# Operands placed by their byte address, and four stage borders rearranged, in a hybrid encoder layer

## The chip, the core and the metric

The kernel runs on one core of a Trainium2 chip. The metric is the device time of one execution, in microseconds. TensorE (PE in the profile) multiplies, VectorE (DVE), ScalarE (ACT) and GpSimd (POOL) work element by element, SyncE (SP) mostly issues DMAs. Every engine has its own instruction queue, and they meet through semaphores.

## What is computed

One layer of a bidirectional encoder on 1280 tokens of width 1024 (1024 sample tokens and 256 prompt tokens), all in float32. Cut to what matters here:

```python
h  = rmsnorm(x, norm_mix)
q, k, v, g, r_f, r_b, aq, ak, av, z_a, z_b = split(h @ w_in)
o_a = gated_linear_attention(q, k, v, g, log_sigmoid(r_f @ w_gk_f + b_gk_f), log_sigmoid(r_b @ w_gk_b + b_gk_b))
o_b = attention(rope(rmsnorm(aq)), rope(rmsnorm(ak)), av)
merged = sigmoid(z_a) * (o_a @ w_o_gla) + sigmoid(z_b) * (o_b @ w_o_att)
x  = x + merged @ w_out
ht = rmsnorm(x, norm_ffn)
gate, idx = top_k(softmax(ht @ w_router).T, 2 * T / 16)     # each of 16 experts picks its tokens
xe  = ht[idx]
ye  = (silu(xe @ w_e_gate) * (xe @ w_e_up)) @ w_e_down * gate
y   = x + scatter_add(idx, ye)
```

r_f and r_b, 16 columns each, are called codes in the kernel.

## The kernel before

The stages run one after another, each in a block of its own with a barrier of all engines at its end: `project` (h and h @ w_in, 0 to 534 us of the profiled span), `gla` (534 to 932, with the z columns of w_in multiplied in between), `mix` with the tag mg (o_a @ w_o_gla, to 1058), `attention` (to 1348), `mix` with the tag ma (to 1464), `finish_mixer` (fm, to 1620), `choose` (tk, the top-k lists, to 1656) and `experts` (ex, to 3135). Names in the profile carry the stage's tag, as pj_w_hi or ex_xS.

A product that has to be exact to float32 is made of three passes: each factor is split into a high part in a type that TensorE takes at full rate (F32R, 4 bytes per element) and a low part, the rest. ACT writes the high part (a copy), DVE the low part (a subtraction), and PE multiplies high by high, high by low and low by high (`three_passes`, L107 to L111, and `channel_tile`, L114 to L131). act_hl holds both parts of the activations of all 1280 tokens. In token tiles (in `project`, the z work and `experts`) 128 tokens are the stationary operand and up to 512 weight columns move past it; in channel tiles (`channel_tile`) 128 weight columns stand still and the tokens move in blocks of 512, 512 and 256 (TOK3).

Where a tensor lies in SBUF follows from the sizes of what was allocated ahead of it: `Phase.sb` (L59) and `program` (L2220 on) take the next free multiple of 32 bytes from the left, or from the right end for those with side="right". Each tensor has the same address in all 128 partitions.

What orders the work around the change:

- `project`: PE ends with the codes, three blocks of tokens, then one ACT copy takes all of them out of PSUM (L412). SP's queue stores every tile and at its end waits for the stores.
- `gla`: SP's queue starts with `gate_weights(0)`, four small DMAs (L1113, L1114), `load_z(0)`, `load_qk(0)` and `ph.start(sp)`, for which other engines wait.
- `mix` mg: rows of o_a^T come in one by one into four buffers (two of them loaded ahead, in `gla`), ACT writes the high part of row k (L901), DVE the low part (L971), and PE's tile 0 waits for each row's low part (`ready` in `channel_tile`). SP loads row k again into the buffer of row k - 4 when its low part is done.
- `choose`: DVE makes the lists (its last step is L1896, slots_i); the first gather of tokens is Pool's first work in the block of `experts` behind it (`gather`, L1989 and L1993).
- `experts`: per expert Pool gathers the next expert's tokens, waits for the sample result (dve_s) and the prompt result (dve_p), and adds both to the output with indirect DMAs (L2010), y for the sample tokens first, then y_q. Weights come in through 8 raw buffers on SP's queue; ACT and DVE split them for the sample tokens (L2024, L2069), while the prompt tokens are multiplied with the raw weights (L2167).

```python
                gate_weights(0)
                load_z(0)
                load_qk(0)
                ph.start(sp)
```

Of the kernel before, what the change touches and what calls it, by code (L numbers as in the profile page):

```python
# [7 lines left out]
ALU = mybir.AluOpType  # L8
# [8 lines left out]
P = 128  # L17
# [33 lines left out]

class Phase:

    def __init__(self, nc, ctx, tag):
# [58 lines left out]
def channel_tile(pe, banks, w, act, full, ready=None, by_columns=False):  # L114
# [8 lines left out]
    for k in range(KC):  # L123
        if ready is not None:
            pe.wait_ge(ready, CR + k + 1)
# [13 lines left out]
def project(nc, x, w_cols, norm_mix, qk_norms, cos, sin, cst, ident, ident_in, act_hl, proj_t, proj_c, codes, ss):  # L139
# [3 lines left out]
    with ExitStack() as ctx:  # L143
# [8 lines left out]
        whi, wlo = ph.sb("w_hi", [P, 2, KC, UW], F32R), ph.sb("w_lo", [P, 2, KC, UW], F32R)  # L152
        rraw = ph.sb("r_raw", [P, KC, RC])
        rhi, rlo = ph.sb("r_hi", [P, KC, RC], F32R), ph.sb("r_lo", [P, KC, RC], F32R)
# [25 lines left out]
        squares = ph.sb("squares", [P, D])[:]  # L180
# [13 lines left out]
        with nc.Block() as block:  # L194

            @block.sync
            def _(sp):
# [117 lines left out]
            def _(act):  # L315
                def square(n, s, i):
# [3 lines left out]
                    act.activation(squares, xt[:, s], ACT.Square, accum_out=ssq[:, s:s + 1]).then_inc(squared, 1)  # L320
# [90 lines left out]
                act.wait_ge(p_full, CR + tok_n + chan_n + 1)  # L411
                act.activation(codes[:], ps_c[0:RC, 0].rearrange("p c n -> p (c n)")[:, 0:T], ACT.Copy).then_inc(p_out, 1)  # L412
# [62 lines left out]
            def _(pe):  # L475
# [60 lines left out]
                mm.then_inc(p_full, 1)  # L536
# [4 lines left out]
def attention(nc, proj_t, inv, cst, kT, vv, queries, act_hl, w_next, w_unit, w_landed):  # L541

    with ExitStack() as ctx:
        ph = Phase(nc, ctx, "at")
        qT = ph.sb("qT", [P, 2, AH, P], F32R)
        pT = ph.sb("pT", [P, 2, 2, NTS, 2, P], F32R)
# [236 lines left out]
def mix(nc, tag, act_hl, w, w_unit, z_rows, out, add=None, o=None, stored=None, source=None, rows_in=None, before=None, keys=None, follow=None, prepare=None):  # L784

    with ExitStack() as ctx:
        ph = Phase(nc, ctx, tag)
        raw, *whl = ([first, ph.sb(n, [P, KC, P], d)[:]] for first, n, d in zip(w_unit, ("w_raw", "w_hi", "w_lo"), (F32, F32R, F32R)))
# [22 lines left out]
        block_gated, block_done = ph.done("block_gated", "block_done")  # L811
# [7 lines left out]
        with nc.Block() as block:  # L819
# [54 lines left out]
            def _(act):  # L874
# [48 lines left out]
            def _(dve):  # L923
# [44 lines left out]
                if source is not None:  # L968
                    for k in range(KC):
                        dve.wait_ge(rows_hi, CR + k + 1)  # L970
                        dve.tensor_tensor(act_hl[:, 1, k], rows[k % NR], act_hl[:, 0, k].bitcast(F32), ALU.subtract).then_inc(rows_lo, 1)  # L971
# [36 lines left out]
            def _(pe):  # L1008
                for t, s in tiles:
# [3 lines left out]
                                 lambda j, k, a, b: act_hl[:, j, k, a:b], full, rows_lo if source is not None and t == 0 else None, by_columns=t == NT8 - 1)  # L1013
# [12 lines left out]
def gla(nc, proj_t, proj_c, z_c, o_t, w_z, wg, bg, g_norm, masks, codes, cst, act_hl, zraw, zw, w_next, qk, rows_in):  # L1026

    with ExitStack() as ctx:
        ph = Phase(nc, ctx, "gl")  # L1030
        v, g = ph.sb("v", [P, NT, DV]), ph.sb("g", [P, NT, DV])
        wgate, bias = ph.sb("w_gate", [3 * RANK, 2, DK]), ph.sb("bias", [P, 2])
# [15 lines left out]
        oss, oroot, oinv = (ph.sb(n, [P, 2]) for n in ("oss", "oroot", "oinv"))  # L1048
# [10 lines left out]
        const_in, qk_in, g_in, w_in, z_in = (ph.landed(n) for n in ("const_in", "qk_in", "g_in", "w_in", "z_in"))  # L1059
# [47 lines left out]
        with nc.Block() as block:  # L1107

            @block.sync
            def _(sp):  # L1110
                def gate_weights(i):
                    for d in range(2):
                        sp.dma_start(wgate[2 * RANK * d:2 * RANK * d + RANK, d], wg[d][:, bass.ds(i * DK, DK)]).then_inc(w_in, 16)  # L1113
                        sp.dma_start(bias[:, d:d + 1], bg[d].rearrange("o (p u) -> (o p) u", u=1)[bass.ds(i * DK, DK)]).then_inc(w_in, 16)  # L1114

# [22 lines left out]
                def body(i, last):  # L1138
                    m = 1 + ZM * i
                    if not last:  # L1140
                        sp.wait_ge(ring_out, CR + RING0 + RING * i)
                        gate_weights(i + 1)
# [52 lines left out]
                gate_weights(0)  # L1195
# [421 lines left out]
def finish_mixer(nc, x, merged, raw, w_in, first_parts, first_tile, merged_stored, norm_ffn, w_router, cst, y, h2, affT, vals, lists, idx):  # L1617

    with ExitStack() as ctx:
# [3 lines left out]
        whl = [(first, ph.sb(n, [P, KC, D // 2], F32R)) for first, n in zip(first_parts, ("w_hi", "w_lo"))]  # L1623
# [212 lines left out]
def choose(nc, affT, cst, vals, lists, idx, slots_i, slots_g, slots_q, start_counts, start_weights, first_high):  # L1836
# [4 lines left out]
    with ExitStack() as ctx:  # L1841
# [10 lines left out]
        with nc.Block() as block:  # L1852
# [45 lines left out]

            @block.scalar
# [12 lines left out]
def experts(nc, affT, vals, lists, idx, h2, y, w_gate, w_up, w_down, slots_i, slots_g, slots_q, cst):  # L1912

    with ExitStack() as ctx:
# [7 lines left out]
        raw = ph.sb("w_raw", [P, NRAW, 2, HF])  # L1923
        whl = [ph.sb(n, [P, NHL, 2, HF], F32R) for n in ("w_hi", "w_lo")]
# [29 lines left out]
        choose(nc, affT, cst, vals, lists, idx, slots_i, slots_g, slots_q, ph.start, start_weights, first_high)  # L1954
# [8 lines left out]
        with nc.Block() as block:  # L1963
# [22 lines left out]
            def _(pool):  # L1986
                def gather(e):
                    for j in range(2):
                        pool.tensor_copy(rows_x[j][:], slots_i[j][:, bass.ds(e, 1)]).then_inc(row_x, 1)  # L1989
                    pool.wait_ge(row_x, CR + 2 * e + 2)  # L1990
                    ph.settle(pool)
                    for j in range(2):
                        pool.indirect_dma_start(xe[j][:], None, h2, bass.IndirectOffsetOnAxis(ap=rows_x[j][:, 0:1], axis=0)).then_inc(x_in[j], 16)  # L1993

# [337 lines left out]
```

## Time and profile before

| | us |
|---|---|
| median of 3 executions | 3151.28 |
| lowest, highest | 3151.15, 3152.47 |
| the profiled execution | 3151.37 |
| its span, first to last instruction | 3149.8 |
| PE busy in the span | 3021.8 (96%) |
| DVE, ACT, POOL busy | 1715.3, 1521.5, 560.9 |
| mean granted clock of TensorE | 0.981 of full speed |

The span is the profiled execution without what lies around it, 1.6 us. A busy engine is one that has an instruction in flight; for PE two matmuls overlap in the records, so that a matmul's own duration is longer than the distance between the starts of two of them, and a span that is 96% busy says nothing about how fast the matmuls follow each other.

### The profile page before, as it was taken

How to read it: one execution, taken by the hardware profiler on the slowest of the kernel's cores; microseconds unless marked ns; L12 is line 12 of the kernel's file. 1: busy time of each engine (PE TensorE's matmuls, PEld its weight loads, DVE VectorE, ACT ScalarE, POOL GpSimd, SP SyncE). 2: the span in 40 equal slices, each digit the busy share in tenths (PEclk: the TensorE clock that was granted, in tenths of full speed). 3: DMA queues.
4: the chain of work that ended last, by engine and by line, in shares of the span. 5: the costliest groups of instructions: out<-in, count | busy, mean ns of one | idle time of the engine just before them, and what ended most of it. 6: DMA issues, size and time to landing. Idle time of an engine off the chain costs nothing. (4 is left out here: it accounts for less than half of the span.)

```text
span 3149.8 us, 51649 instructions
## 1 busy us (share of the span) xinstructions
PE 3021.8 (96%) x19370; PEld 2391.6 (76%) x19370; DVE 1715.3 (54%) x1748; ACT 1521.5 (48%) x1659; POOL 560.9 (18%) x729
## 2 busy tenths in 40 slices
PE   8999999999989999999949999999999999999998
PEld 6888886777778799878837777777777777777776
DVE  4101000555443599924367676666667676666665
ACT  4211111455632366622435665655666665556554
POOL 0048883112220000011100111000111100111100
PEclk9999999999999999999969999999999999999999
DMA  5224323233335100063447887778888778888874
GB/s 184 105 99 143 121 90 103 96 111 115 95 111 195 55 20 20 7 227 135 160 163 260 296 285 273 276 284 293 293 296 293 270 274 299 284 289 291 293 273 146
DMA packets 196414, 600.32 MB, mean 191 GB/s; under 512 B 15392, under 2 KB 45744, under 8 KB 196336
## 3 DMA queue, kind: packets, MB, share of 16 engines
q1 hardware_dynamic: 166144, 508.03, 44.9%
q0 software_dynamic: 21328, 73.41, 7.8%
q10 hardware_dynamic: 8864, 17.83, 1.6%
q8 instruction: 50, 0.82, 0.1%
q14 instruction: 28, 0.23, 0.0%
HBM read 521.80 MB, written 77.33 MB: 190 GB/s over the span
## 5 line engine op out<-in xcount | busy, mean ns | idle before, releaser
L2069 DVE TENSOR_TENSOR ex_w_lo<-ex_w_raw,ex_w_hi 128x2048 fp32r<-128x2048 f32 x384 | 880.0, 2292 | 451.1 <-ACT ex_w_hi L2024 451.1
L2024 ACT ACTIVATE ex_w_hi<-ex_w_raw 128x2048 fp32r<-128x2048 f32 x381 | 729.9, 1916 | 469.6 <-PE ex_ps_s L2156 469.5
L2156 PE MATMUL ex_ps_s<-ex_w_hi,ex_xS 128*128 128x512 f32 x2048 | 578.5, 396 | 0.0
L2156 PEld LDWEIGHTS ex_ps_s<-ex_w_hi,ex_xS 128*128 128x128 f32 x2048 | 376.2, 188 | 99.1 <-issue 26.3
L2156 PE MATMUL ex_ps_s<-ex_w_lo,ex_xS 128*128 128x512 f32 x1024 | 316.7, 390 | 0.0
L2156 PE MATMUL ex_ps_s<-ex_w_hi,ex_hidS 128*128 128x512 f32 x1024 | 308.1, 403 | 0.0
L2010 POOL DMA_INDIRECT y<-ex_ye_s,ex_rows_y x16 | 43.7, 2729 | 1147.1 <-DVE ex_ye_s L2112 1147.1
L2167 PE MATMUL ex_ps_p<-ex_w_raw,ex_xP 128*32 128x256 f32 x4096 | 236.1, 383 | 0.0
L2156 PEld LDWEIGHTS ex_ps_s<-ex_w_lo,ex_xS 128*128 128x128 f32 x1024 | 192.4, 188 | 41.3
L109 PE MATMUL pj_ps_tok<-pj_w_hi,act_hl 128*128 128x512 f32 x560 | 219.9, 393 | 2.4 <-DVE act_hl L436 2.4
L111 PE MATMUL pj_ps_tok<-pj_w_hi,act_hl 128*128 128x512 f32 x560 | 218.9, 391 | 0.0
L110 PE MATMUL pj_ps_tok<-pj_w_lo,act_hl 128*128 128x512 f32 x560 | 218.9, 391 | 0.0
L2156 PEld LDWEIGHTS ex_ps_s<-ex_w_hi,ex_hidS 128*128 128x128 f32 x1024 | 183.0, 188 | 46.6 <-issue 13.2
L2167 PEld LDWEIGHTS ex_ps_p<-ex_w_raw,ex_xP 128*32 128x32 f32 x4096 | 127.2, 110 | 100.5 <-issue 24.3
L453 DVE TENSOR_TENSOR pj_w_lo<-pj_w_raw,pj_w_hi 128x4096 fp32r<-128x4096 f32 x7 | 32.9, 4697 | 300.4 <-ACT pj_w_hi L363 300.4
L368 ACT ACTIVATE pj_stage<-pj_ps_tok 128x512 f32<-128x512 f32 x70 | 41.9, 598 | 287.3 <-PE pj_ps_tok L111 287.3
L2156 PE MATMUL ex_ps_s<-ex_w_lo,ex_hidS 128*128 128x512 f32 x512 | 159.6, 393 | 0.0
L109 PE MATMUL gl_z_ps<-act_hl,z_w_hi 128*128 128x512 f32 (+1 forms) x384 | 152.0, 396 | 0.4 <-issue 0.4
L111 PE MATMUL gl_z_ps<-act_hl,z_w_lo 128*128 128x512 f32 (+1 forms) x384 | 138.2, 360 | 0.0
L110 PE MATMUL gl_z_ps<-act_hl,z_w_hi 128*128 128x512 f32 (+1 forms) x384 | 137.7, 358 | 0.0
L109 PEld LDWEIGHTS pj_ps_tok<-pj_w_hi,act_hl 128*128 128x128 f32 x560 | 105.7, 189 | 24.9 <-DVE act_hl L436 3.1
L111 PEld LDWEIGHTS pj_ps_tok<-pj_w_hi,act_hl 128*128 128x128 f32 x560 | 105.6, 189 | 22.0
(334 smaller groups left out, 5140.1 us busy)
## 6 DMA issues: line engine op xcount, KB each, us to landing
ex_w_raw<-w_e_gate SPq DMA_DIRECT2D x128, 1024.0 KB, 11.3
ex_w_raw<-w_e_up SPq DMA_DIRECT2D x128, 1024.0 KB, 11.7
ex_w_raw<-w_e_down SPq DMA_DIRECT2D x128, 1024.0 KB, 8.7
proj_t<-pj_stage SPq DMA_DIRECT2D x60, 256.0 KB, 2.1
pj_w_raw<-w_cols ACTq DMA_DIRECT2D x7, 2048.0 KB, 8.8
z_w_raw<-w_z SPq DMA_DIRECT2D x16, 512.0 KB, 4.0
gate_logits<-gl_z_stage SPq DMA_DIRECT2D x32, 256.0 KB, 2.1
pj_w_raw<-x SPq DMA_DIRECT2D x10, 512.0 KB, 3.7
```

Source lines behind the costliest of these rows:

```text
L109: pe.matmul(out, a[0], b[0], start=first, stop=False)
L110: pe.matmul(out, a[0], b[1], start=False, stop=False)
L111: return pe.matmul(out, a[1], b[0], start=False, stop=last)
L368: act.activation(stage[:, s, 0:width], src, ACT.Copy).then_inc(p_out, 1)
L453: dve.tensor_tensor(wlo[:, s], raw[:, s], whi[:, s].bitcast(F32), ALU.subtract).then_inc(w_lo, 1)
L2010: pool.indirect_dma_start(dst, bass.IndirectOffsetOnAxis(ap=rows_y[j][:, 0:1], axis=0), src[:], None, compute_op=ALU.add).then_inc(scatter ...
L2024: act.activation(whl[0][:, j % NHL], raw[:, j % NRAW], ACT.Copy).then_inc(w_hi, 1)
L2069: dve.tensor_tensor(whl[1][:, j % NHL], raw[:, j % NRAW], whl[0][:, j % NHL].bitcast(F32), ALU.subtract).then_inc(w_lo, 1)
L2156: mm = pe.matmul(ps_s[:, s, c:c + 512], x(part, k), whl[w][:, j % NHL, kk, c:c + 512], start=k == 0 and part + w == 0, stop=k == 2 * PU - ...
L2167: mm = pe.matmul(ps_p[CP * c:CP * c + CP, f % 2, 0:QW], x(k, c), raw[:, j % NRAW, k % 2, QW * c:QW * c + QW], start=k == 0, stop=k == 2 * ...
```

## The change

1. **Places.** `place` puts every tensor of at least 512 bytes per partition at a chosen offset within 128 bytes, with a gap tensor ahead of it where needed: activations at 0 (AT), weights and other partners of a product at 64 (AT_W; also kT and pT in `attention`). The right end is shifted so that the tensors there lie at 64. `gla`'s own tensors are packed as before (lines=False). To free space `project` loses its buffer squares (the Square writes into xn instead, behind one more wait) and `gla` merges three small tensors.
2. **Codes by blocks.** PE reports each of the three code blocks, and ACT copies each by itself.
3. **First gate weights.** The four DMAs of `gate_weights(0)` go into `project`'s SP queue, behind its last store and ahead of its last waits.
4. **Row 0 by blocks.** In mg ACT and DVE split row 0 in three column blocks, and PE takes row 0 block by block, all three passes of a block together.
5. **First gather.** It goes into a Pool block of `choose`, behind a wait for the last list.
6. **Scatter.** The prompt's scatter goes first as soon as dve_p is there, then the sample's on dve_s.

The core of the diff:

```diff
@@ placement
+BYTES = {F32: 4, F32R: 4, U32: 4, BF16: 2, U8: 1}
+LINE, AT, AT_W = 128, 0, 64
+
+def place(nc, ctx, name, shape, dt=F32, at=AT):
+    size = math.prod(shape[1:]) * BYTES[dt]
+    if size >= 512 and at is not None:
+        gap = (at - (nc.sbuf_base + 31) // 32 * 32) % LINE
+        if gap:
+            ctx.enter_context(nc.sbuf_tensor(f"gap_{name}", [P, gap // 4], F32))
+    return ctx.enter_context(nc.sbuf_tensor(name, shape, dt))
+
 class Phase:
-    def sb(self, name, shape, dt=F32):
-        return self.ctx.enter_context(self.nc.sbuf_tensor(f"{self.tag}_{name}", shape, dt))
+    def sb(self, name, shape, dt=F32, at=AT):
+        return place(self.nc, self.ctx, f"{self.tag}_{name}", shape, dt, at if self.lines else None)
@@ project
-        whi, wlo = ph.sb("w_hi", [P, 2, KC, UW], F32R), ph.sb("w_lo", [P, 2, KC, UW], F32R)
+        whi, wlo = ph.sb("w_hi", [P, 2, KC, UW], F32R, AT_W), ph.sb("w_lo", [P, 2, KC, UW], F32R, AT_W)
...
+                first_gates(sp, 0)
                 for s in range(2):
                     sp.wait_ge(stored[s], ST + 16 * (tok_n + chan_n) // 2)
...
+                    act.wait_ge(turned, CR + n - 1)
-                    act.activation(squares, xt[:, s], ACT.Square, accum_out=ssq[:, s:s + 1]).then_inc(squared, 1)
+                    act.activation(xn[:, s], xt[:, s], ACT.Square, accum_out=ssq[:, s:s + 1]).then_inc(squared, 1)
...
-                act.wait_ge(p_full, CR + tok_n + chan_n + 1)
-                act.activation(codes[:], ps_c[0:RC, 0].rearrange("p c n -> p (c n)")[:, 0:T], ACT.Copy).then_inc(p_out, 1)
+                for c, (a, b) in enumerate(TOK3):
+                    act.wait_ge(p_full, CR + tok_n + chan_n + c + 1)
+                    act.activation(codes[:, a:b], ps_c[0:RC, 0, c, 0:b - a], ACT.Copy).then_inc(p_out, 1)
...
-                mm.then_inc(p_full, 1)
+                    mm.then_inc(p_full, 1)
@@ channel_tile, mix
+        if ready is not None and k == 0:
+            for c, (a, b) in enumerate(TOK3):
+                pe.wait_ge(ready[0] if b < T else ready[1], CR + c + 1 if b < T else CR + 1)
+                three_passes(pe, banks[:, c, 0:b - a], (w(0, k), w(1, k)), (act(0, k, a, b), act(1, k, a, b)), True, False)
+            continue
...
-                        act.activation(act_hl[:, 0, k], rows[k % NR], ACT.Copy).then_inc(rows_hi, 1)
+                        for c, (a, b) in enumerate(TOK3 if k == 0 else [(0, T)]):
+                            act.activation(act_hl[:, 0, k, a:b], rows[k % NR][:, a:b], ACT.Copy).then_inc(rows_hi if b == T else row0_hi, 1)
...
+                        for c, (a, b) in enumerate(TOK3 if k == 0 else [(0, T)]):
+                            dve.wait_ge(rows_hi if b == T else row0_hi, CR + k + 1 if b == T else CR + c + 1)
+                            dve.tensor_tensor(act_hl[:, 1, k, a:b], rows[k % NR][:, a:b], act_hl[:, 0, k, a:b].bitcast(F32),
+                                              ALU.subtract).then_inc(rows_lo if b == T else row0_lo, 1)
@@ gla
-        ph = Phase(nc, ctx, "gl")
+        ph = Phase(nc, ctx, "gl", lines=False)
...
-                gate_weights(0)
                 load_z(0)
                 load_qk(0)
                 ph.start(sp)
@@ choose, experts
+            @block.gpsimd
+            def _(pool):
+                pool.wait_ge(out, CR + 10)
+                first_gather(pool, 0)
...
-        raw = ph.sb("w_raw", [P, NRAW, 2, HF])
-        whl = [ph.sb(n, [P, NHL, 2, HF], F32R) for n in ("w_hi", "w_lo")]
+        raw = ph.sb("w_raw", [P, NRAW, 2, HF], F32, AT_W)
+        whl = [ph.sb(n, [P, NHL, 2, HF], F32R, AT_W) for n in ("w_hi", "w_lo")]
...
-                    pool.wait_ge(dve_s, CR + 3 * e + 3)
-                    pool.wait_ge(dve_p, CR + 3 * e + 3)
-                    ph.settle(pool)
-                    for j, (dst, src) in enumerate(((y, yS), (y_q, yP))):
+                    for j, dst, src, ready in ((1, y_q, yP, dve_p), (0, y, yS, dve_s)):
+                        ph.settle(pool)
+                        pool.wait_ge(ready, CR + 3 * e + 3)
+                        ph.settle(pool)
                         pool.indirect_dma_start(dst, bass.IndirectOffsetOnAxis(ap=rows_y[j][:, 0:1], axis=0), src[:], None,
                                                 compute_op=ALU.add).then_inc(scattered[j], 16)
...
-                gather(0)
                 experts_of(pool, body)
@@ program
+        gap = (nc.sbuf_top - AT_W) % LINE
+        if gap:
+            ctx.enter_context(nc.sbuf_tensor("gap_right", [P, gap // 4], F32, side="right"))
...
-            act_hl = mixer.enter_context(nc.sbuf_tensor("act_hl", [P, 2, KC, T], F32R))
             ss = mixer.enter_context(nc.sbuf_tensor("head_squares", [P, NT, HEADS], F32))
+            act_hl = place(nc, mixer, "act_hl", [P, 2, KC, T], F32R)
...
-                kT = kvs.enter_context(nc.sbuf_tensor("kT", [P, 2, KVH, T], F32R))
-                vv = kvs.enter_context(nc.sbuf_tensor("vv", [P, 2, NT, KVH * HD], F32R))
+                kT = place(nc, kvs, "kT", [P, 2, KVH, T], F32R, AT_W)
+                vv = place(nc, kvs, "vv", [P, 2, NT, KVH * HD], F32R)
```

In the same way AT_W is given to pj_r_hi and r_lo, at_pT, the `mix` weights, fm's w_hi and w_lo; the other tensors named in `program` (codes, w_gate, gate_bias, head_inverses, q_rows, affT, aff, lists, idx) go through `place` with AT.

## Rows read from the trace of the kernel before

**Rows 1.** Stages: stretch us, busy us of PE PEld DVE ACT POOL, PEclk, DMA share, GB/s.

```profile
549.00:932.00 383.00, 362.29 (x1844) 295.39 (x1843) 196.51 (x357) 205.10 (x351) 74.67 (x84) 0.99 0.31 101
932.00:952.00 20.00, 13.53 (x54) 10.90 (x54) 9.65 (x7) 8.79 (x7) 2.15 (x4) 0.74 0.85 325
1058.00:1348.00 290.00, 271.14 (x1874) 243.48 (x1872) 256.85 (x462) 186.92 (x382) 22.26 (x18) 0.98 0.07 21
1656.00:3135.00 1479.00, 1479.00 (x11314) 1098.30 (x11312) 1019.09 (x622) 880.06 (x603) 149.18 (x154) 1.00 0.79 280
```

**Rows 2.** Timeline of PE: start us, duration us, line, operands; token part of project.

```profile
200.33 0.39 PE L109 MATMUL pj_ps_tok<-pj_w_hi,act_hl 128*128 128x512 f32 x1
...
205.77 0.39 PE L109 MATMUL pj_ps_tok<-pj_w_hi,act_hl 128*128 128x512 f32 x1
```

**Rows 3.** Chain that ended last, the 20 longest pieces: start us, length us, what.

```profile
1661.71 11.10 PE ex_ps_s L2156 x48
```

**Rows 4.** Groups by form in experts: busy us, mean ns of one, idle before.

```profile
L2156 PE MATMUL ex_ps_s<-ex_w_hi,ex_xS 128*128 128x512 f32 x2048 | 578.5, 396 | 0.0
L2156 PE MATMUL ex_ps_s<-ex_w_lo,ex_xS 128*128 128x512 f32 x1024 | 316.7, 390 | 0.0
L2156 PE MATMUL ex_ps_s<-ex_w_hi,ex_hidS 128*128 128x512 f32 x1024 | 308.1, 403 | 0.0
...
L2156 PE MATMUL ex_ps_s<-ex_w_lo,ex_hidS 128*128 128x512 f32 x512 | 159.6, 393 | 0.0
```

**Rows 5.** Timeline of PE, last tile of the first mix.

```profile
1043.98 0.39 PE L109 MATMUL mg_ps<-act_hl,mg_w_hi 128*128 128x512 f32 x1
...
1046.78 0.40 PE L109 MATMUL mg_ps<-act_hl,mg_w_hi 128*128 128x512 f32 x1
```

**Rows 6.** Timeline of PE, last tile of the second mix.

```profile
1449.38 0.40 PE L110 MATMUL ma_ps<-act_hl,ma_w_hi 128*128 128x512 f32 x1
...
1451.48 0.39 PE L110 MATMUL ma_ps<-act_hl,ma_w_hi 128*128 128x512 f32 x1
```

**Rows 7.** Timeline of PE, scores in attention.

```profile
1199.89 0.39 PE L109 MATMUL at_ps_scores<-kT,at_qT 128*128 128x512 f32 x1
...
1201.06 0.40 PE L111 MATMUL at_ps_scores<-kT,at_qT 128*128 128x512 f32 x1
```

**Rows 8.** Groups by form, token part of project (one of three passes).

```profile
L109 PE MATMUL pj_ps_tok<-pj_w_hi,act_hl 128*128 128x512 f32 x560 | 219.9, 393 | 2.4 <-DVE act_hl L436 2.4
```

**Rows 9.** Timeline of all engines, project to gla; idle time before and its releaser in brackets.

```profile
533.73 1.23 ACT L412 ACTIVATE codes<-pj_ps_chan 48x1280 f32<-48x1280 f32 x1 [10.92 <-PE pj_ps_chan L111]
535.84 0.37 SPq L1113 DMA_DIRECT2D gl_w_gate<-w_gk_f  x1
...
537.65 0.43 SPq L1125 DMA_DIRECT2D z_w_raw<-w_z  x1
...
539.47 1.19 PE L1499 MATMUL gl_ring<-codes,gl_w_gate 16*128 16x512 f32 x1 [5.78 <-SPq L84]
```

**Rows 10.** Timeline of all engines, tile 0 of the first mix.

```profile
952.76 1.43 PE L128 MATMUL mg_ps<-act_hl,z_w_hi 128*128 128x512 f32 x6 [1.43 <-DVE act_hl L971]
953.01 1.27 ACT L901 ACTIVATE act_hl<-mg_row 128x1280 fp32r<-128x1280 f32 x1 [1.83 <-DMA mg_row<-gla_out]
```

**Rows 11.** Timeline of all engines, choose to experts.

```profile
1646.02 0.17 DVE L1896 TENSOR_TENSOR slots_i<-tk_diff,tk_b 128x16 uint32<-128x16 f32 x1
1647.11 0.29 POOL L1989 COPY ex_rows_x<-slots_i 128x1 uint32<-128x1 uint32 x2 [67.57 <-POOLq L96]
...
1649.67 0.89 POOL L1993 DMA_INDIRECT ex_xe<-h,ex_rows_x  x1 [0.30 <-issue]
...
1653.42 1.03 PE L2130 MATMUL ex_ps_t<-identity,ex_xe 32*128 32x32 f32 x8 [8.72 <-DMA ex_xe<-h,ex_rows_x]
```

**Rows 12.** Timeline of all engines, the end.

```profile
3137.35 1.59 POOL L2010 DMA_INDIRECT y<-ex_ye_s,ex_rows_y  x1 [72.46 <-DVE ex_ye_s L2112]
3139.24 1.55 POOL L2010 DMA_INDIRECT y<-ex_ye_p,ex_rows_y  x1 [0.30 <-issue]
```

More of the change, by code:

```diff
@@ L1 @@
+import math
 from contextlib import ExitStack
@@ L123, in channel_tile @@
     for k in range(KC):
+        if ready is not None and k == 0:
[3 more added lines that the diff above has]
+            continue
         if ready is not None:
-            pe.wait_ge(ready, CR + k + 1)
+            pe.wait_ge(ready[1], CR + k + 1)
         for part, other in ((0, 0), (0, 1), (1, 0)):
@@ L136, in pairs, with project @@
     return t.rearrange("... (d e) -> ... d e", e=2)[..., e]
-def project(nc, x, w_cols, norm_mix, qk_norms, cos, sin, cst, ident, ident_in, act_hl, proj_t, proj_c, codes, ss):
+def project(nc, x, w_cols, norm_mix, qk_norms, cos, sin, cst, ident, ident_in, act_hl, proj_t, proj_c, codes, ss, first_gates):
     with ExitStack() as ctx:
@@ L787, in mix @@
         ph = Phase(nc, ctx, tag)
-        raw, *whl = ([first, ph.sb(n, [P, KC, P], d)[:]] for first, n, d in zip(w_unit, ("w_raw", "w_hi", "w_lo"), (F32, F32R, F32R)))
+        raw, *whl = ([first, ph.sb(n, [P, KC, P], d, AT_W)[:]] for first, n, d in zip(w_unit, ("w_raw", "w_hi", "w_lo"), (F32, F32R, F32R)))
         z = ph.sb("z", [P, 2, T])
@@ L1012, in _ @@
                     channel_tile(pe, ps[:, s], lambda j, k: whl[j][s][:, k],
-                                 lambda j, k, a, b: act_hl[:, j, k, a:b], full, rows_lo if source is not None and t == 0 else None, by_columns=t == NT8 - 1)
+                                 lambda j, k, a, b: act_hl[:, j, k, a:b], full, (row0_lo, rows_lo) if source is not None and t == 0 else None, by_columns=t == NT8 - 1)
                     if 1 <= t <= pairs_n:
@@ L1047, in gla @@
         o_n = flat[:, 2 * P:2 * P + 2 * DV].rearrange("p (s n) -> p s n", s=2)
-        oss, oroot, oinv = (ph.sb(n, [P, 2]) for n in ("oss", "oroot", "oinv"))
+        o_sums = ph.sb("o_sums", [P, 3, 2])
+        oss, oroot, oinv = (o_sums[:, j] for j in range(3))
         oT = ph.sb("o_turned", [P, 2, 2, P])
@@ L1058, in gla @@
         o_ps = u_ps
-        const_in, qk_in, g_in, w_in, z_in = (ph.landed(n) for n in ("const_in", "qk_in", "g_in", "w_in", "z_in"))
+        const_in, qk_in, g_in, z_in = (ph.landed(n) for n in ("const_in", "qk_in", "g_in", "z_in"))
+        w_in = gates_in
         v_in = ph.landed("v_in", 2)
@@ L1110, in _ @@
             def _(sp):
[L1111 to L1114, printed above, removed]
                 def load_qk(i):
@@ L1622, in finish_mixer @@
         NU = D // WC
-        whl = [(first, ph.sb(n, [P, KC, D // 2], F32R)) for first, n in zip(first_parts, ("w_hi", "w_lo"))]
+        whl = [(first, ph.sb(n, [P, KC, D // 2], F32R, AT_W)) for first, n in zip(first_parts, ("w_hi", "w_lo"))]
         wr, gamma = ph.sb("w_router", [P, KC, NE]), ph.sb("gamma", [P, D])
@@ L1952, in first_high, with gather @@
                 act.activation(whl[0][:, j], raw[:, j], ACT.Copy).then_inc(w_hi, 1)
-        choose(nc, affT, cst, vals, lists, idx, slots_i, slots_g, slots_q, ph.start, start_weights, first_high)
+        def gather(pool, e):
+            for j in range(2):
+                pool.tensor_copy(rows_x[j][:], slots_i[j][:, bass.ds(e, 1)]).then_inc(row_x, 1)
+            pool.wait_ge(row_x, CR + 2 * e + 2)
+            ph.settle(pool)
+            for j in range(2):
+                pool.indirect_dma_start(xe[j][:], None, h2, bass.IndirectOffsetOnAxis(ap=rows_x[j][:, 0:1], axis=0)).then_inc(x_in[j], 16)
+        choose(nc, affT, cst, vals, lists, idx, slots_i, slots_g, slots_q, ph.start, start_weights, first_high, gather)
         ps_s, ps_p, ps_t = ph.ps("ps_s", [P, 2, HF]), ph.ps("ps_p", [P, 2, 512]), ph.ps("ps_t", [P, 2, 512])
@@ L1999, in body @@
                         pool.wait_ge(turned, CR + XT + TURNS * e)
-                        gather(e + 1)
+                        gather(pool, e + 1)
                     for j, src in enumerate(slots_g):
@@ L2272, in program @@
         with ExitStack() as router:
[L2273 to L2276 removed]
+            affT = place(nc, router, "affT", [NE, T], F32)
+            vals = place(nc, router, "aff", [ROWS, TS // 2], F32)
+            lists = place(nc, router, "lists", [ROWS, 4, CS], F32)
+            idx = place(nc, router, "idx", [ROWS, CS], U32)
             with shared_rows, out_stage:
```

50 lines of the change are left out of this document (22 added, 28 removed).

## The prediction

> **What bounds the kernel now.** I read the stage table first [rows 1]: it shows for each stretch of the span how much of it TensorE was multiplying. In `experts`, 1479 us and nearly half of everything, PE is busy 1479.00 of 1479.00 us at a granted clock of 1.00, so at its 2.4 GHz level, with the DMA engines at 0.79. Nothing but the matmuls themselves is worth anything there. `gla` (362.29 of 383) and `attention` (271.14 of 290) leave a few per cent to others; at the entry of the first `mix` (13.53 of 20, clock 0.74) and at the other stage borders [rows 9, 11, 12] PE waits. So the change has two halves: a step of a few us at four stage borders, and one number, the distance from one matmul's start to the next, multiplied by thousands.
>
> That number is not the duration in the grouped view (about 390 ns, since two matmuls overlap); it has to be taken from starts. In the token part of `project` 24 steps lie between the two starts shown [rows 2]: (205.77 - 200.33)/24 = 226.7 ns. At 2.4 GHz 512 columns take 512/2.4 = 213.3 ns, so 13.3 ns, 32 cycles, are lost on each. In `experts` a run of 48 on the chain takes 11.10 us [rows 3], so at most 231 ns each; the four groups [rows 4] sum to 2048 + 1024 + 1024 + 512 = 4608 such matmuls.
>
> **Part one: the addresses.** Adding up the sizes in the code, every operand of these two streams begins 96 bytes past a multiple of 128, stationary and moving alike. The trace of before has three other pairs, by (stationary, moving): (32, 96) in the last tile of the first `mix`, (1046.78 - 1043.98)/12 = 233.3 ns [rows 5]; (0, 96) in the last tile of the second, (1451.48 - 1449.38)/9 = 233.3 ns [rows 6]; and (32, 0) in the scores, (1201.06 - 1199.89)/5 = 234 ns [rows 7]. So the place of the operands does show in the time, and equal offsets are the best pair there so far, by 6.7 ns. The change makes all pairs (0, 64) or (64, 0): at distance 64 like [rows 5], but, other than every pair in this trace, with both operands on a multiple of 64.
>
 Then 2048 bytes that begin 32 bytes behind a multiple of 64 touch 33 such pieces, from a multiple of 64 they touch 32, and each matmul at the locked step (34) would need one step less: 33 x 6.67 = 220.0 ns. I take 220 for the new pair. Bounds: below, the 213.3 ns of the columns alone; above, the 233.3 ns of the other pairs [rows 5 to 7]. 220 is one step from the nearest long stream [rows 2], and by the piece count the only step that the alignment itself removes.
>
> The sum, at 6.67 ns each. Where PE is the bound: experts 4608 [rows 4], token part 3 x 560 = 1680 [rows 8], and by the code 384 in the channel part of `project` and 384 in each `mix`: 7440 x 6.67 = 49.6 us. Where PE is busy only 93 to 95% [rows 1] (by the code the z work in `gla`, 768, and the scores, 384; and in `finish_mixer`, 480) I count half: 1632 x 6.67 / 2 = 5.4 us. The 256-column matmuls are left at nothing; the 576 in the channel tiles could be worth 576 x 6.67 = 3.8 us. Together -55 us. At the lower bound it is 7440 x 13.3 + 5.4 x 2 = -110 us; at the upper see the first rival. The cover does not run out: with 31 us less in `experts` the DMA share goes from 0.79 to 0.79 x 1479/1448 = 0.81, and DVE is busy 1019 of 1479 [rows 1]. ACT and DVE read and write the moved tensors too; no row bears on their speed by address, and with 30 to 40% idle in `experts` I price it at nothing, some 10 us either way if it reached the path. The gap tensors cost space, no time.
>
> The Trainium skill ("TensorE: Matmul & The Clock Gate", section "Back-to-back issue gap") gives a gap of 512/2.4 + 2.5, some 216 ns, with no word on addresses; no stream of 512 columns here reaches it, the trace has 226.7 and more. By it, as an estimate, the same counts would give 7440 x 10.7 = 80 us.
>
> **Part two: the borders.** *`project` to `gla`.* After the last code matmul ACT copies 48x1280 in 1.23 us from 533.73; SP starts the four gate transfers at 535.84, and z_w_raw follows at 537.65, 1.81 us later; the first ring matmul, waiting for SP's start, begins at 539.47 after 5.78 us of idleness [rows 9]. With three copies only the last, 48x256, remains behind the last matmul; no row has one, by size it lies between nothing and a fifth of 1.23 plus a fixed part, so I take 0.38 and a gain of 0.85 (bounds 0.6 to 1.0). The four issues move to SP's queue in `project`, behind the last channel store and ahead of the waits for the stores. ACT was idle for 10.92 us before the code copy [rows 9], so the last store is out some 10 us earlier and the 1.8 us are hidden; if they were not, SP would reach the border late by as much and the gain would be nothing. Behind them load_z, load_qk and ph.start move up by 1.81. Together -2.7 us (0 to -3). The split copies' two more increments cost PE nothing: they ride on matmuls.
>
> *Row 0 by blocks.* PE could start on a third of row 0 about 1.5 us earlier. But tile 0 is paced by what lands: PE waits for row 6's low part until 952.76, that for ACT, and ACT sat idle for 1.83 us before row 7 at 953.01 for its DMA [rows 10], with DMA at 0.85 in that stretch [rows 1]. The early start is given back: 0 (bounds -1.5 and +0.3, for two more small instructions on ACT and on DVE ahead of the load that reuses row 0's buffer).
>
> *First gather.* Pool's copy at 1647.11 starts 0.92 us after the last routing step (1646.02 + 0.17), with a block border between; PE's first transpose waits 8.72 us for the gathered rows and begins at 1653.42 [rows 11]. Ahead of the barrier Pool waits on the semaphore alone: -0.8 us (0 to -0.9). Behind it in Pool's queue is only the barrier, so the other engines now wait there for Pool's two issues, the last of them 1649.67 + 0.89 - 0.8 = 1649.8, and a border of 0.9 more: 1650.7, before the rows land (1653.42 - 0.8) [rows 11].
>
> *Last scatter.* After the last DVE step Pool issues y at 3137.35 (1.59 us) and then y_q at 3139.24 [rows 12]. y_q is ready long before and now goes first, so the end waits for y alone: -0.7 us (0 to -1.9, the distance of the two issues). In all other experts Pool waits for DVE anyway, so the added settles cost nothing.
>
> The Square that now writes into xn waits for turned, which the step before it has waited for: 0. Sum of the borders -4.2 us (+0.3 to -7).
>
> **The forecast.** The profiled run took 3151.37 us for a span of 3149.8, 0.09 above the median of 3151.28. 3151.4 - 55 - 4.2 = 3092 us, for a pitch of 220. Its own range, 216 to 223 ns and the borders, is 3050 to 3125.
>
> **Rival one, slower: the distance decides, not the alignment.** All three pairs at unequal offsets run at 233 ns whatever their absolute place, and having the moving operand at 0 gave the scores nothing [rows 5 to 7]. If a distance of 64 is what costs, the locked streams go from 226.7 to 233.3: token part 1680 x 6.67 = +11.2 us; experts between 4608 x 2 ns = +9 (from 231) and 4608 x 6.67 = +31 (from 226.7), middle 20; the rest about 2. With the borders 3151.4 + 33 - 4.2 = 3180 us (3167 to 3191). It decides from the first matmul and would show in the token part alone. For it: three rows. Against: each of those pairs has an operand off a multiple of 64.
>
> **Rival two: no net effect of the places.** Either the piece that alignment saves and the one that distance 64 costs cancel, or the loss has another cause. The locked streams then stay at 226.7 and only the borders are left, 3147 us; if the unlocked stretches, `experts` among them, come down to 226.7 as well, by 2 to 4 ns on 4608, some 3131. The Trainium skill, same page, section "Step-by-step: what each phase is for", says that PE has two independent read ports and that loading weights takes no bandwidth from a running matmul; by that the pair's distance could not matter, and the addresses would be worth nothing. The differences between [rows 2] and [rows 5 to 7] speak against it.
>
> **Chances.** Forecast 0.44, rival two 0.24, rival one 0.27; 0.05 for something else (ACT or DVE, or a border gone wrong). A measurement of this kernel can tell about 0.2%, 6 us. Faster by more: 0.44 + half of rival two + a little of the rest, 0.58; within it 0.14; slower 0.28. The range takes the forecast's own nearly whole, rival two, and rival one's lower half: 3050 to 3180.
>
> **What would show it.** Starts in the token part: 24 steps in 5.28 us (220), 5.44 (no change) or 5.60 (rival one); runs of 48 in `experts` at 10.6, 10.9 to 11.1, or 11.2 us. First ring matmul 2.7 us closer to the last code matmul; the matmuls of row 0 earlier but tile 0's end unmoved; first transposes 6.4 instead of 7.2 us after the last routing step; one scatter behind the last DVE step. Wrong would be above all the reading of 6.67 ns as a piece of 64 bytes.

## The result: slower, by the places

The changed kernel takes 3174.94 us (median of 4 runs, 3172.36 to 3175.78) against 3151.88 us before: a ratio of 1.0075, with a 95% interval of 1.0063 to 1.0087. The profiled execution took 3172.36 us for a span of 3170.8.

Where the span grew by 21.0 us, from the first to the last matmul of each stage and the idle time of PE between them:

| | before us | after us | difference |
|---|---|---|---|
| project | 524.0 | 526.2 | +2.2 |
| idle to gla | 5.78 | 3.01 | -2.8 |
| gla | 391.5 | 394.6 | +3.1 |
| idle to mix mg | 6.60 | 5.22 | -1.4 |
| mix mg | 120.6 | 122.0 | +1.4 |
| attention | 286.0 | 285.7 | -0.3 |
| mix ma | 114.5 | 113.3 | -1.1 |
| finish_mixer | 153.5 | 152.9 | -0.6 |
| idle choose to experts | 8.72 | 8.79 | +0.1 |
| experts | 1481.8 | 1502.7 | +20.9 |
| last matmul to the end | 14.58 | 13.84 | -0.7 |

So the borders moved by a few us, and one stage has the loss. `experts` is full of matmuls as before; each of them follows later. Two starts 24 matmuls apart in the token part of `project` (before in [rows 2]), and below them a run of 48 in `experts` on the chain that ended last (before in [rows 3]), both of the changed kernel; the timeline's columns are start, duration, line and operands, the chain's start and length:

```profile
199.64 0.39 PE L125 MATMUL pj_ps_tok<-pj_w_hi,act_hl 128*128 128x512 f32 x1
...
205.13 0.39 PE L125 MATMUL pj_ps_tok<-pj_w_hi,act_hl 128*128 128x512 f32 x1
```

```profile
1676.51 11.39 PE ex_ps_s L2181 x48
```

(205.13 - 199.64)/24 = 228.8 ns in `project`, against 226.7. The run of 48 takes 11.39 us against 11.10; from the starts of the matmuls inside all such runs the mean is 233.3 ns against 227.1. For all 4608 matmuls 20.9 us are 4.5 ns each, less than the 6.2 ns between those two means, because the loss is not the same everywhere: from first to last start each of the 49 runs of 48 is 0.28 us longer (13.9 us in all), each of the 188 runs of 12 between them only 0.037 us (6.9 us).

The borders of the changed kernel, which answer to [rows 9] (`project` to `gla`), [rows 10] (tile 0 of the first mix), [rows 11] (`choose` to `experts`) and [rows 12] (the end), from its timeline; in brackets the idle time before and its releaser:

```profile
525.63 0.37 SPq L2276 DMA_DIRECT2D w_gate<-w_gk_f  x1
...
535.83 0.38 ACT L435 ACTIVATE codes<-pj_ps_chan 48x256 f32<-48x256 f32 x1 [2.17 <-PE pj_ps_chan L127]
537.09 0.33 SPq L1147 DMA_DIRECT2D z_w_raw<-w_z  x1
...
538.80 2.60 PE L1520 MATMUL gl_ring<-codes,w_gate 16*128 16x512 f32 x3 [3.02 <-SPq L100]
```

```profile
955.26 1.43 PE L149 MATMUL mg_ps<-act_hl,z_w_hi 128*128 128x512 f32 x6 [1.66 <-DVE act_hl L996]
955.59 1.27 ACT L925 ACTIVATE act_hl<-mg_row 128x1280 fp32r<-128x1280 f32 x1 [1.90 <-DMA mg_row<-gla_out]
```

```profile
1646.76 0.17 DVE L1917 TENSOR_TENSOR slots_i<-tk_diff,tk_b 128x16 uint32<-128x16 f32 x1
1647.00 0.29 POOL L1982 COPY ex_rows_x<-slots_i 128x1 uint32<-128x1 uint32 x2 [66.74 <-DVE slots_i L1917]
...
1649.55 0.89 POOL L1986 DMA_INDIRECT ex_xe<-h,ex_rows_x  x1 [0.30 <-issue]
...
1654.23 1.03 PE L2155 MATMUL ex_ps_t<-identity,ex_xe 32*128 32x32 f32 x8 [8.79 <-DVEq L112]
```

```profile
3156.98 1.28 DVE L2137 SCALAR_TENSOR_TENSOR ex_ye_s<-ex_ps_s,ex_gate,ex_ye_s 128x1024 f32<-128x1024 f32 x1 [9.35 <-PE ex_ps_s L2181]
3159.06 1.55 POOL L2036 DMA_INDIRECT y<-ex_ye_s,ex_rows_y  x1 [9.04 <-DVE ex_ye_s L2137]
```

The gate transfers start at 525.63, 10 us ahead of the end of the codes, and the last code copy takes 0.38 us; z_w_raw follows 0.9 us behind it. In the first mix PE still waits for the last rows, and the stage is longer by what it began earlier. Pool's first gather starts 0.07 us after the last list, where it took 0.92 us before, and yet PE's first transpose comes 7.30 us after that list against 7.23, and now what releases it is no longer the rows' landing but a barrier. At the end only one scatter stands behind the last DVE step.

### The profile page after: what moved, and what is told of

Same layout as the page of the kernel before. It is cut to its first block and busy times, and to the rows that moved or that the text cites. A ratio compares the mean times of both kernels' runs of the same rounds, so it can differ in the third digit from the quotient of the medians.

```text
span 3170.8 us, 51716 instructions
## 1 busy us (share of the span) xinstructions
PE 3043.4 (96%) x19370; PEld 2386.3 (75%) x19370; DVE 1717.1 (54%) x1750; ACT 1521.9 (48%) x1663; POOL 545.2 (17%) x729
## 5 line engine op out<-in xcount | busy, mean ns | idle before, releaser
L2181 PE MATMUL ex_ps_s<-ex_w_hi,ex_xS 128*128 128x512 f32 x2048 | 589.2, 401 | 0.0
L2036 POOL DMA_INDIRECT y<-ex_ye_p,ex_rows_y x16 | 25.8, 1615 | 993.6 <-DVE ex_ye_p L2128 993.6
```

What stands on the lines that cost most here:

```text
L2036: pool.indirect_dma_start(dst, bass.IndirectOffsetOnAxis(ap=rows_y[j][:, 0:1], axis=0), src[:], None, compute_op=ALU.add).then_inc(scatter ...
L2181: mm = pe.matmul(ps_s[:, s, c:c + 512], x(part, k), whl[w][:, j % NHL, kk, c:c + 512], start=k == 0 and part + w == 0, stop=k == 2 * PU - ...
```

## The experiments

Three theories went in. D: what counts is the distance between the stationary and the moving operand, and distance 0 is best. S: the same, but counted with its sign and modulo 256 bytes; it came from the changed kernel itself, whose places modulo 128 were the same in both stages but modulo 256 were not: in `project` the stationary operand lies 64 below the moving one (128 and 192 of 256), in `experts` 64 above it (128 and 64). A: the forecast's own, by which it counts that an operand starts on a multiple of 64. Distances below are stationary less moving, modulo 256, and operands are given as (stationary, moving).

All these kernels are the changed one with other places. This diff is common to them; the numbers in PLACES (for `project` and what follows it) and PLACES_EX (for `experts`) change from run to run, and one run counts modulo 512:

```diff
-LINE, AT, AT_W = 128, 0, 64
+LINE, AT, AT_W = 256, 0, 1
+PLACES, PLACES_EX, RIGHT = (224, 224), (224, 224), 224
...
-        gap = (at - (nc.sbuf_base + 31) // 32 * 32) % LINE
+        gap = (places[at] - (nc.sbuf_base + 31) // 32 * 32) % LINE
...
-        return place(self.nc, self.ctx, f"{self.tag}_{name}", shape, dt, at if self.lines else None)
+        return place(self.nc, self.ctx, f"{self.tag}_{name}", shape, dt, at if self.lines else None,
+                     PLACES_EX if self.tag == "ex" else PLACES)
...
-        gap = (nc.sbuf_top - AT_W) % LINE
+        gap = (nc.sbuf_top - RIGHT) % LINE
```

head_squares is allocated behind act_hl again, and codes and w_gate take the next free place. The tensors at the right end (z_w, att_w, w_out, merged) lie at 224 modulo 256 in all of them, act_hl too.

**All at 224.** PLACES and PLACES_EX are (224, 224).

> The changed kernel with every operand at 224 of 256 bytes (96 of 128), so at distance 0 everywhere; the border edits stay. Theory D (the distance of stationary and moving operand sets the pitch, distance 0 is best): token part of project at 226.7 ns, runs of 48 in experts at 11.10 us, the mix stages somewhat faster than before because their odd tiles were at other distances; time 3144 to 3149 us, so before less about 2.8 (project to gla) and 0.7 (last scatter) and some us of mix. Theory A (alignment to 64 bytes): the same pitch as before, since nothing is aligned. If the places were not what cost the 23 us, it would stay near 3172.

Measured: 3150.98 us against 3151.06 of before on the same chip, ratio 1.000 (0.9991 to 1.0010). With the border edits kept and only the places changed, the 23 us are gone. The starts of the token part and a run of 48 of this kernel:

```profile
199.79 0.39 PE L129 MATMUL pj_ps_tok<-pj_w_hi,act_hl 128*128 128x512 f32 x1
...
205.23 0.39 PE L129 MATMUL pj_ps_tok<-pj_w_hi,act_hl 128*128 128x512 f32 x1
```

```profile
1674.85 11.10 PE ex_ps_s L2183 x48
```

226.7 ns and 11.10 us, as before. The last tile of the first mix, which stood at 233.3 ns in [rows 5], came to 227.5 by the mean of its starts, now that its operands are at distance 0 as well. So the places are the cause, as D and S have it. A expected this pitch here too, since nothing is aligned, so between A and the others this run does not decide. The time lies 2 us above its expectation of 3144 to 3149. In its profile `project` is 526.5 us long, 2.5 more than before, at the same pitch; the run without the Square's wait, below, takes that up.

**Project at +64, experts aligned at 0.** PLACES (224, 160), PLACES_EX (0, 0).

> Project's stationary operand 64 bytes above the moving one (mod 256), both 32 off a multiple of 64; experts with both operands at 0 of 256, aligned and at distance 0. Theory D: experts' runs of 48 at 11.10 us as before; theory A: about 10.6 us (220 ns) or less. Project under a distance counted mod 256 with its sign (theory S, from the changed kernel: experts at +64 give 233.3, project at -64 gives 229.0): 233.3 ns, 5.60 us for 24 steps; under a distance mod 128 without sign: 229.0 as in the changed kernel. Time: S 3159, A about 3120 to 3130.

Measured: 3159.17 us, ratio 1.0025 (1.0016 to 1.0035).

```profile
199.62 0.39 PE L127 MATMUL pj_ps_tok<-pj_w_hi,act_hl 128*128 128x512 f32 x1
...
205.22 0.39 PE L127 MATMUL pj_ps_tok<-pj_w_hi,act_hl 128*128 128x512 f32 x1
```

```profile
1683.74 11.10 PE ex_ps_s L2183 x48
```

This run decided against A: with both operands on a multiple of 256 a run of 48 takes 11.10 us, to the hundredth what it took at 224. And it decided for the sign: `project` at +64 has 5.60/24 = 233.3 ns, where the changed kernel at -64 had 228.8.

**Project and experts at -64.** PLACES (224, 32), PLACES_EX (0, 64).

> Project at distance -64 as in the changed kernel but both operands moved by 32 (224 and 32 of 256, not aligned); experts at -64 instead of +64, both aligned (0 and 64). Theory S: project 229.0 ns as in the changed kernel, experts 229 ns, so runs of 48 at about 11.18 us instead of 11.39; time about 3160. Without sign: experts stay at 11.39 us, time 3170 to 3175. Theory A: project slower than 229.0, since it lost its alignment.

Measured: 3158.96 us, ratio 1.0026 (1.0016 to 1.0036).

```profile
199.76 0.39 PE L127 MATMUL pj_ps_tok<-pj_w_hi,act_hl 128*128 128x512 f32 x1
...
205.26 0.39 PE L127 MATMUL pj_ps_tok<-pj_w_hi,act_hl 128*128 128x512 f32 x1
```

```profile
1753.28 11.21 PE ex_ps_s L2183 x48
```

`experts` has its operands at 0 and 64 modulo 128, as in the changed kernel, only on the other side of each other modulo 256, and a run of 48 takes 11.21 instead of 11.39 us. `project` has its distance of the changed kernel with both operands 32 bytes off, and keeps its 229 ns: alignment counts for nothing.

**Experts at +64, off by 32; project at +32.** PLACES (224, 192), PLACES_EX (224, 160).

> Experts at +64 as in the changed kernel, but both operands 32 off a multiple of 64 (224 and 160 of 256). Theories D and S: runs of 48 at 11.39 us as in the changed kernel; theory A: another pitch, slower. Project at +32, a distance not seen so far in the token part: D without further knowledge 227 to 233 ns. Time 3165 to 3180.

Measured: 3183.89 us, ratio 1.0103 (1.0086 to 1.0119), a little above the expectation; `project` at +32 took 233.3 ns, the upper end of what was left open.

```profile
1813.43 11.39 PE ex_ps_s L2183 x48
```

11.39 us, as in the changed kernel, with unaligned operands.

**The other distances.** Each of these kernels has two of them, one for each stage; their times are those of one execution. PLACES (224, 96) and PLACES_EX (0, 128):

> Distance 128 of 256 in project (unaligned) and in experts (aligned). If the distance counts mod 128, this is distance 0: 226.7 ns in the token part and runs of 48 at 11.10 us in experts. If it counts mod 256 (theory S), another pitch than 226.7, the same in both stages; in the changed kernel's finish_mixer the one pair at 128 had about 232 ns, so 232 to 233 and 11.35 us.

PLACES (224, 0) and PLACES_EX (0, 224):

> Experts at +32, which gave project 233.3 ns in the run before: theory S says runs of 48 at 11.39 us. Project at -32, not seen so far: between 226.7 and 233.3 ns. A distance that is better than 0 would show as 24 steps in less than 5.44 us.

PLACES (224, 128) and PLACES_EX (0, 32):

> Experts at -32: theory S says the pitch that project shows at -32 in the run beside it. Project at +96, not seen so far in a token part: between 226.7 and 233.3 ns.

PLACES (480, 64) and PLACES_EX (0, 256), counted modulo 512 (LINE 512, RIGHT 480):

> Experts with the moving weights 256 bytes from the stationary tokens, mod 512. If the period is 256 this is distance 0: runs of 48 at 11.10 us; if it is 512 or more, another pitch. Project at -96, the distance of the second mix and of the scores before, which ran at 233 ns: theory S says about 233.

Measured: 3176.36, 3178.94, 3186.21 and 3161.17 us, against 3151.51 of before. The runs of 48 at distances 128 and 256:

```profile
1762.62 11.36 PE ex_ps_s L2183 x48
```

```profile
1686.30 11.10 PE ex_ps_s L2183 x48
```

At 256 it is 11.10 us again, at 128 it is 11.36: the period is 256 bytes, not 128. All distances together, as the mean from start to start in long runs of 512 columns (from the starts in the traces; the rows above are samples of them):

| stationary less moving, mod 256 | project, ns | experts, ns |
|---|---|---|
| 0 | 226.8 | 227.1 (at 224, at 0, and 256 apart) |
| +32 | 233.3 | 233.3 |
| +64 | 233.3 | 233.3 (aligned or not) |
| +96 | 234.3 | not run |
| 128 | 232.4 | 232.7 |
| -96 | 233.4 | not run |
| -64 | 229.0 (aligned or not) | 229.1 |
| -32 | 233.3 | 233.4 |

No distance beats 0. Wherever both stages ran at one distance, they agree within 0.4 ns, though one takes its weights from a tensor that stays and the other from buffers that are filled anew all the time. The last tile of each mix, 48 matmuls of 512 columns, gives a third and a fourth place: in the eight runs above it agrees with the table at all eight distances, within 0.8 ns. With triples of 512, 512 and 256 columns (the channel tiles) it is the other way round: 586.5 ns from one triple to the next at 0 and at -64, but 580 at +64, in the channel part of `project`, in both mixes, before and after. That is why the second mix became shorter, by 1.1 us.

**The gather undone.** All at 224, with the first gather back in `experts`.

```diff
-            @block.gpsimd
-            def _(pool):
-                pool.wait_ge(out, CR + 10)
-                first_gather(pool, 0)
...
+                gather(pool, 0)
                 experts_of(pool, body)
```

> The kernel with everything at 224 of 256 bytes, its first gather back in experts' own block. In the changed kernel Pool's drain at choose's end lasts 4.87 us, until the gathered rows have landed, and the barriers come after it. If that took the 0.85 us of the earlier start back, the idle time between the last routing product and the first transpose stays where it is, 8.7 to 8.8 us (8.72 before, 8.83 with the gather moved). If moving the gather did bring something, it is 0.8 us longer here.

Measured: 3150.53 us in one execution. PE's first transpose, first of this kernel, then of the one with all at 224 and the gather moved:

```profile
1653.14 1.03 PE L2153 MATMUL ex_ps_t<-identity,ex_xe 32*128 32x32 f32 x8 [8.78 <-DMA ex_xe<-h,ex_rows_x]
```

```profile
1652.58 1.03 PE L2157 MATMUL ex_ps_t<-identity,ex_xe 32*128 32x32 f32 x8 [8.83 <-DVEq L114]
```

8.78 us with the gather behind the barrier, 8.83 ahead of it: the move brings nothing. Only the releaser changes, from the rows to a barrier.

**Row 0 whole.** All at 224, `TOK3 if k == 0 else [(0, T)]` cut to `[(0, T)]` on ACT and DVE, and PE's branch for k = 0 taken out.

> Everything at 224 of 256 bytes, row 0 of the first mix whole again. If tile 0 is paced by the rows' landing, PE starts 1.4 us later (idle 6.6 us instead of 5.2) and the stage is shorter by as much or more: idle plus stage 127 to 128 us against 128.1 with row 0 by blocks. If the early start was worth something, the sum is 129 us or more.

Measured: 3149.09 us in one execution. The idle time before the stage is 6.59 instead of 5.22 us, the stage 121.6 instead of 122.9; together 128.2 against 128.1. The start of tile 1 in this kernel, and in the one with row 0 by blocks:

```profile
934.84 2.47 PE L146 MATMUL mg_ps<-act_hl,z_w_hi 128*128 128x512 f32 x6 [6.59 <-DVE act_hl L993]
...
955.89 1.33 PE L146 MATMUL mg_ps<-act_hl,mg_w_hi 128*128 128x512 f32 x6
```

```profile
933.63 0.77 PE L127 MATMUL mg_ps<-act_hl,z_w_hi 128*128 128x512 f32 x1 [5.22 <-SPq L102]
...
955.90 1.33 PE L151 MATMUL mg_ps<-act_hl,mg_w_hi 128*128 128x512 f32 x6
```

Tile 0 starts 1.21 us earlier by blocks and tile 1 at the same moment. The early start is given back within the tile.

**The Square without its wait.** All at 224; the Square of `project` writes into a buffer that only Pool uses, and only later.

```diff
-        row_buf = [gamma[:, 0:HH * HD], ph.sb("h_rows", [P, HH * HD])[:]]
+        h_two = ph.sb("h_rows", [P, 2 * HH * HD])
+        squares = h_two[:, 0:D]
+        row_buf = [gamma[:, 0:HH * HD], h_two[:, 0:HH * HD]]
...
-                    act.wait_ge(turned, CR + n - 1)
-                    act.activation(xn[:, s], xt[:, s], ACT.Square, accum_out=ssq[:, s:s + 1]).then_inc(squared, 1)
+                    act.activation(squares, xt[:, s], ACT.Square, accum_out=ssq[:, s:s + 1]).then_inc(squared, 1)
```

> Everything at 224 of 256 bytes; the Square of project writes into a buffer that only Pool uses, later, so that its wait for the transposes of the tile before goes. If this wait is what makes the beginning of project longer (the 240th token matmul at 83.1 us against 80.6 before), it is back at 80.5 to 80.7 us and project is 2.4 us shorter; time 3147 to 3149 us. If not, 83 us stay.

Measured: 3148.97 us, ratio 0.9994 (0.9985 to 1.0004), no difference from before that can be told. The wait stands in the traces, but by itself it did not make the beginning of `project` longer. ACT's waits in the first 66 us, engine, line, what it waited for, us in total, times, longest; first with all at 224, then in the changed kernel:

```profile
ACT pj_w_raw L344 <- PE pj_ps_chan L505: 2.3, 3, 0.8
```

```profile
ACT pj_w_raw L342 <- PE pj_ps_chan L503: 2.3, 3, 0.8
```

In both the Square (which writes into pj_w_raw there) waits for PE's transposes three times, 2.3 us in all; with the wait gone it waits only for what stands ahead of it on ACT. But the start behind 240 token matmuls is at 83.1 us with all at 224 (82.5 and 83.2 in the two kernels above), at 80.8 in the changed kernel, at 80.6 before and at 80.1 without the wait. What differs is the granted clock. Below, with all at 224, the transposes that PE waits for and the stretch behind their start; then the same stretch of the changed kernel (from and to, its length, busy us of PE PEld DVE ACT POOL, PEclk, DMA share, GB/s):

```profile
38.84 1.23 PE L505 MATMUL pj_ps_chan<-identity,pj_w_raw 128*128 128x128 f32 x8 [2.11 <-DVE pj_w_raw L450]
39.70:43.10 3.40, 3.40 (x11) 2.73 (x9) 1.99 (x4) 2.36 (x4) 0.00 (x0) 0.50 0.86 222
```

```profile
37.90:41.30 3.40, 3.40 (x19) 2.98 (x20) 1.99 (x3) 2.50 (x5) 0.00 (x0) 1.00 0.60 147
```

With all at 224 the clock was at its 1.2 GHz level here, and 24 token matmuls from the 73rd on took 7.9 us; in the changed kernel it stayed at 2.4 GHz, and they took 6.4. PE had been idle for 2.11 and for 2.09 us before these transposes, without the wait for 1.74. In the profiles of the eleven kernels that have the wait the clock fell in seven at this place, in the three that do not (before, this one and the next) in none; in the seven the start behind 240 token matmuls comes after 82.4 us, in all others before 82.1. So it is the clock that took most of the 2.5 us; whether the wait brings the fall about is not shown.

**Three parts undone.** The last three edits together: of the change only the codes by blocks, the first gate weights, the scatter's order, and the placing at one equal offset are left.

> Everything at 224 of 256 bytes, without the Square's wait, row 0 whole, the gather in experts: of the change only the codes by blocks, the first gate weights and the scatter are left, and the equal distances of the mix stages. Gains over before by the traces: 2.8 (project to gla), 0.7 (end), 2 (gla), 1 to 2 (mix and finish_mixer): 3143 to 3146 us, ratio 0.998. A version that beats both kernels; if the borders were worth nothing, 3151.

Measured: 3149.53 us against 3151.07, ratio 0.9995 (0.9986 to 1.0005). It isn't shown to be faster than before, and lies 3.5 us above the upper end of its expectation. The border gains are in its trace (idle to `gla` 3.02 instead of 5.78 us, the end 13.86 instead of 14.58), but the stages between them vary by 1 to 2 us from one profile to the next (`gla` from 389.0 to 393.5 in the five kernels with all at 224), and the gain of 2 us that I expected from `gla` was within that. The granted clock goes with it here too: in the five it was at the 1.2 GHz level for 10.2 and 13.7 us of `gla` where that took 389.3 and 389.0, and for 17.1 and 20.1 us where it took 391.9 and 393.5 (this kernel: 13.7 and 391.0). It beats the changed kernel by 0.8%, not the one before.

## Why the prediction was wrong

**The step that failed** is the one from 6.67 ns to a piece of 64 bytes, and from there to 220 ns. The numbers were right: 226.7 and 233.3 are 34 and 35 times 6.67 ns. But that a matmul at 96 of 128 bytes loses one step to its alignment was only inferred, and the run with both operands at 0 took 11.10 us, as at 224. At distance 0 the operands may lie at a multiple of 64 or not, and at +64 and -64 too: their distance counts. Nor does a pitch go by whole steps of 6.67 ns: the 229.0 and 232.4 ns at other distances are 34.3 and 34.8 of them. The term of -55 us came out, over all stages but without the borders, as some +25 us (the stages of the table above, mix mg's +1.4 of which is the early start given back; `gla`'s +3.1 stands beside z tiles at +64 and more time at the 1.2 GHz level, 20.5 us against 17.9, and no run parts the two). The range (3050 to 3180) holds 3174.94 only because it took in the lower half of rival one; the forecast of 3092 and the chance of 0.58 for faster were wrong in sign.

**Rival one was right**, with 3180 us for 3174.94 and 233.3 ns in `experts`: +20.9 us there, against the 9 to 31 that it gave, 20 in the middle. That the middle was met is luck: it lies halfway between two readings of the pitch before (231 and 226.7 ns), while the pitch rose by 6.2 ns in the long runs and by half of that in the short ones. It missed in `project`, where it had +11.2 us and it was +2.2: the pitch rose to 229.0, not to 233.3, and 192 triples at 580 instead of 586.5 ns gave 1.2 us back. What it lacked was the period. The code's LINE of 128 and my own adding up of addresses modulo 128 hid that (128, 192) and (128, 64) are different pairs.

**What the rows of before held.** Three pairs at unequal offsets stood at 233 ns [rows 5 to 7] and the two streams at equal offsets at 226.7 and 227.1 [rows 2, 3]. Counted modulo 256 the mix of [rows 6] and the scores of [rows 7] are both at -96: (128, 224) and (32, 128). One has its moving operand on a multiple of 128 and the other does not, and they ran alike. That was the test of alignment, it lay in the rows, and I let a reason for why each pair might not count (one operand off 64) outweigh three measurements.

**Rival two**, no effect of the places, is refuted: every other distance that was run has a longer pitch than 0. The page of the Trainium skill that it named ("TensorE: Matmul & The Clock Gate", section "Step-by-step: what each phase is for") has two independent read ports and no bandwidth taken from a running matmul by the next weight load. By it the distance could not matter. The traces differ: the place of the stationary operand against the moving one changes the pitch by up to 7.5 ns (226.8 to 234.3 in `project`).

**The borders.** *`project` to `gla`*: -2.8 us of idle time, predicted -2.7. The copy took 0.38 us as taken, and the gate transfers lay in the idle time of SP's queue. *Row 0*: 0, as predicted, and in one pair of profiles tile 1 starts at the same moment (955.90 and 955.89). *Last scatter*: -0.7, as predicted. *First gather*: predicted -0.8, measured +0.1. The step that failed is "behind it in Pool's queue is only the barrier". At the end of the block Pool has a drain, recorded from 1648.51 for 4.87 us, until 1653.38: it does not end when the gathers are issued (1649.55 + 0.89 = 1650.44) but about when they have landed (the second 3.7 us after the start of its issue, at 1653.2). The other engines leave two barriers after that, at 1654.1. The 1650.7 of the prediction was 3.4 us early. *The Square*: I put the wait for the transposes at 0, since the step before had waited for the same. The reason was wrong: the Square waits 2.3 us for them on ACT, and PE's idle time at that place is 2.09 us instead of 1.74. In the changed kernel itself the start behind 240 token matmuls came at 80.8 us against 80.6, so there it cost at most little. The 1.8 to 2.5 us that the kernels with all at 224 and the wait are late at that place are for the most part the fall of the granted clock (81.4 in the last kernel, which has neither the wait nor the fall, shows that some 1.3 us also come and go without them).

Left open: why distance 0 is best, and why -64 comes next; distances that are no multiple of 32 were not run. And one place does not fit the table: in the changed kernel the last tile of the first mix is at -64 and ran at 233.3 ns, where another kernel at that distance (project at +64, where the channel tiles are at -64) ran it at 229.1. A distance may have more than one steady rhythm; no run here was made to tell. `gla`'s z tiles do fit. They are channel tiles, not token tiles as the description of the kernel before has it: by the code (`z_part`) z_w stands still and act_hl moves, so in the changed kernel they are at +64, and they ran at 233.1 ns.

## What to carry to other kernels

Where matmuls follow each other without a gap, measure the distance from start to start at the operands' present places before moving them, and compare stretches of the same kernel by their places modulo 256, not by one's idea of a good alignment: three rows that measure outrank a count that fits. An equal offset of stationary and moving operand was best for streams of 512 columns here (for the triples with a block of 256 columns it was not), and it costs nothing but a gap tensor. The two indirect DMAs that Pool issued here ahead of a barrier held the barrier until about their landing, so nothing that stood behind the barrier came earlier. And before a difference of 2 us in a stage is put down to an edit, look at the granted clock in it.

## What was not expected of the hardware

TensorE's pitch for 512 columns of 4 bytes depends on the byte distance of its two operands with a period of 256 bytes and with its sign: 226.8 ns at 0, 229.0 at -64, 232.4 to 234.3 at the six others that were run, the same after both operands are moved together by 32 bytes (run at 0, +64 and -64), and the same at 0 and at 256. In `experts` that is 21 us of 1482, without one instruction added. And Pool's drain at the end of a block waited 2.9 us past the last issue, for two gathers of 0.66 MB in all.
